# An encoder block on one core: the projection's first block in another order, outer products stored by SP, the first head's K and Q loaded at other places

## What is computed

```python
proj = rmsnorm(h, norm1_g) @ w_in                # 1024 -> 2048: q, k, v, u, 512 columns each
lam = exp(sum(lam_q1 * lam_k1)) - exp(sum(lam_q2 * lam_k2)) + 0.2
p = softmax(q_i . k_i * 64**-0.5 - slope_h * |i - j|)            # i = 0, 1: two maps per head
att = rmsnorm((p[0] - lam * p[1]) @ v, subln_g) * 0.8
ssm = bi_s5_glu(u, ...)              # two scans, 32 groups of 64 complex states, then GELU and a gate
h = h + concat(att, ssm) @ w_out
h = h + square(relu(rmsnorm(h, norm2_g) @ w_mlp1)) @ w_mlp2
return rmsnorm(h, final_g)
```

## Time and profile before

| | |
|---|---|
| median of 3 runs | 2672.96 us (2672.41 to 2673.84) |
| the profiled execution | 2665.66 us, its span 2663.5 us |
| PE busy | 2548.7 us, 96% of the span |
| DVE, ACT, POOL busy | 2077.4, 1416.7, 389.5 us |
| DMA | 397.18 MB, mean 149 GB/s |

### The profile page before, as it was taken

How to read it: one execution, slowest core, us unless ns; L and a number is a source line. 1 busy time by engine, 2 the same in 40 slices (tenths; PEclk the granted TensorE clock), 3 DMA queues, 4 the chain that set the end, 5 groups by cost and what they waited for, 6 DMA issues and landing times.

```text
span 2663.5 us, 32920 instructions
## 1 busy us (share of the span) xinstructions
PE 2548.7 (96%) x12804; PEld 2079.2 (78%) x12804; DVE 2077.4 (78%) x2074; ACT 1416.7 (53%) x1753; POOL 389.5 (15%) x333
## 2 busy tenths in 40 slices
PE   7998999999999988988989999999999999999997
PEld 6886777877787877766777888888887888888886
DVE  5866657999999968766998876777889877678885
ACT  5276626777787762224434666533345565643334
POOL 3410021212121113310434000000014000000003
PEclk9999999999999999998999999999999999999999
DMA  5356542020213119966665554452234664452211
GB/s 187 119 188 221 216 136 72 25 64 26 56 39 89 49 41 255 256 220 245 221 236 202 212 206 186 174 205 106 104 109 159 233 221 174 181 198 95 97 78 63
DMA packets 162714, 397.18 MB, mean 149 GB/s; under 512 B 29568, under 2 KB 87168, under 8 KB 134784
## 3 DMA queue, kind: packets, MB, share of 16 engines
q1 hardware_dynamic: 145856, 319.07, 36.1%
q10 hardware_dynamic: 16704, 76.03, 7.2%
HBM read 270.79 MB, written 122.16 MB: 148 GB/s over the span
## 4 chain that ended last, share of the span: by engine, by line
PE 45%; DVE 3%; POOL 1%; issue 1%; DMA 0%; ACT 0%; SPq 0%; DVEq 0%; ACTq 0%; POOLq 0%
PE ml_bank L2590 15%; PE ml_bank L2592 15%; PE ml_bank L2591 15%; POOL kp_tabs L2199 1%; DVE ml_res L2470 1%; DMA kp_low<-hn_s 0%; DVE ml_hb L2504 0%; DVE ml_b_split L2401 0%; DVE ml_w_split L2412 0%; DVE ml_res L2490 0%; DVE ml_rinv L2496 0%; PE ml_bank L2598 0%; DVE kp_low L2425 0%; DVE kp_tabs L2446 0%; DVE ml_t_first L2419 0%
## 5 line engine op out<-in xcount | busy, mean ns | idle before, releaser
L2590 PE MATMUL ml_bank<-ml_b_split,ml_w_split 128*128 128x512 f32 x2016 | 788.8, 391 | 9.7 <-issue 9.4
L2591 PE MATMUL ml_bank<-ml_b_split,ml_w_split 128*128 128x512 f32 x2016 | 786.1, 390 | 0.0
L2592 PE MATMUL ml_bank<-ml_b_split,ml_w_split 128*128 128x512 f32 x2016 | 785.9, 390 | 0.0
L2590 PEld LDWEIGHTS ml_bank<-ml_b_split,ml_w_split 128*128 128x128 f32 x2016 | 379.5, 188 | 93.2 <-issue 14.1
L2591 PEld LDWEIGHTS ml_bank<-ml_b_split,ml_w_split 128*128 128x128 f32 x2016 | 379.6, 188 | 79.9 <-issue 1.2
L2592 PEld LDWEIGHTS ml_bank<-ml_b_split,ml_w_split 128*128 128x128 f32 x2016 | 379.6, 188 | 79.1
L1065 ACT ACTIVATE at_e<-at_e,at_neg_top 128x2048 f32<-128x2048 f32 x128 | 256.5, 2004 | 143.2 <-DVE at_neg_top L1119 143.2
L2199 POOL TENSOR_TENSOR kp_tabs<-kp_tabs,ml_square 128x512 f32<-128x512 f32 x55 | 144.2, 2622 | 1265.8 <-ACT ml_square L2303 1259.3
L2470 DVE TENSOR_TENSOR ml_res<-ml_bank,ml_res 128x2048 f32<-128x2048 f32 x75 | 171.5, 2287 | 118.7 <-PE ml_bank L2592 118.7
L2237 ACT ACTIVATE ml_b_split<-kp_u_t 128x2048 fp32r<-128x2048 f32 x54 | 103.5, 1917 | 300.5 <-PE ml_bank L2592 300.5
L1221 PEld LDWEIGHTS pj_banks<-at_v,at_a_t 128*128 128x128 f32 x2048 | 238.6, 192 | 22.8 <-issue 22.6
(11 more groups left out here) (227 smaller groups left out, 4057.3 us busy)
## 6 DMA issues: line engine op xcount, KB each, us to landing
act_s<-ml_res ACTq DMA_DIRECT2D x32, 1024.0 KB, 4.2
kp_wide<-in_w_stream SPq DMA_DIRECT2D x18, 1024.0 KB, 5.1
kp_bp<-in_w_stream SPq DMA_DIRECT2D x18, 1024.0 KB, 5.8
kp_tabs<-in_w_stream SPq DMA_DIRECT2D x18, 1024.0 KB, 6.7
ml_r<-in_w_stream SPq DMA_DIRECT2D x18, 1024.0 KB, 6.8
tab_s<-kp_tabs ACTq DMA_DIRECT2D x32, 512.0 KB, 3.0
kp_low<-hn_s SPq DMA_DIRECT2D x16, 1024.0 KB, 5.6
kp_u_t<-hn_s SPq DMA_DIRECT2D x16, 1024.0 KB, 4.8
```

What stands on the lines that cost most here:

```text
L2590: pe.matmul(out, w_hi[:, w], b_hi[:, b], start=fresh and kt == 0, stop=False, skip_group_check=True)
L2591: pe.matmul(out, w_hi[:, w], b_lo[:, b], start=False, stop=False, skip_group_check=True)
L2592: last = pe.matmul(out, w_lo[:, w], b_hi[:, b], start=False, stop=kt == 3, skip_group_check=True)
```

## The change

It has five parts.

1. **Opening.** ACT runs a small activation before it waits for data. The first slice of x is a DMA of its own ahead of the first weight piece, and is split first. PE runs eight matmuls of 128 by 128 on the constant `ones`.
2. **Block 0.** Strip 1 of x is loaded behind weight piece 6 instead of ahead of it. ACT takes the inverse norm's root (`stats(0)`) after piece 6, and splits piece 7 in the middle of block 1's squares; DVE splits piece 7 after the evacuation of group 1. `rates` and `chunk_turns` move from groups 2 and 3 to ahead of `invert(0)`, `magnitudes` to behind the split of x for block 1.
3. **Outer products** are stored by SP, right behind the store of their own group.
4. **First K.** It is loaded behind group 53's store into the first half of `e`, and ACT splits it in one run with Q 0 and 1 before it evacuates group 56; DVE's `first_k_low`, the biases and the lambda exponents move two or one groups ahead.
5. **Q 2 and 3** are issued behind group 62's store; the wait for all stores of u moves into attention, ahead of the first load of u.

```diff
     def store_outer(self, sp, i):
-        act.wait_ge(self.outer_ready, i + 1)
+        sp.wait_ge(self.outer_ready, i + 1)
 ...
+        sp.dma_start(x_raw[:, 0], x_tiles[:, 0, 0:TB]).then_inc(x_first_loaded, 16)
         load_w(0)
-        load_half_x(0, 0)
+        sp.dma_start(x_raw[:, 1:KD // 2], x_tiles[:, 1:KD // 2, 0:TB]).then_inc(x_loaded[0], 16)
 ...
-            if i == HALF_W - 2:
+            if i == HALF_W - 1:
                 load_x(1)
 ...
             store(n)
-            if n == NG - 8:
+            if n in PREP_OUTERS:
+                prep.store_outer(sp, PREP_OUTERS.index(n))
+            if n == NG - 11:
 ...
+            if n == NG - 2:
+                for tile in range(2, 4):
+                    attention.load_q(sp, tile)
 ...
-        for i in range(2):
-            sp.wait_ge(qku_stored[i], 16 * (SECOND + NV * NTB) // 2)
 ... (ACT)
+        act.activation(rms_t[:, 0:1], eps_c[:], ACT.Copy)
+        split_x(0, range(1))
         split_w(0)
-        split_x(0)
+        split_x(0, range(1, KD))
 ...
+        prep.time_steps(act)
+        split_w(6)
         stats(0)
-        prep.time_steps(act)
-        squares(1, range(KD))
-        prep.magnitudes(act)
+        squares(1, range(KD // 2))
+        split_w(7)
+        squares(1, range(KD // 2, KD))
 ...
+            if n == NGROUP - 1:
+                prep.magnitudes(act)
 ...
-            if n == NG - 7:
+            if n == NG - 9:
                 prep.all_used(act)
-                attention.k_high(act, 0, range(4))
+                attention.q_high(act, 0)
+                attention.k_high(act, 0, range(8))
+                attention.q_high(act, 1)
 ...
-            if n - 2 in PREP_OUTERS:
-                prep.store_outer(act, PREP_OUTERS.index(n - 2))
 ... (DVE)
-        for i in range(1, HALF_W):
+        for i in range(1, HALF_W - 1):
             split_w(i)
+        prep.rates(dve)
+        prep.chunk_turns(dve)
         invert(0)
 ...
+            if n == 1:
+                split_w(HALF_W - 1)
 ... (PE)
+        for i in range(8):
+            pe.matmul(stat_b[:, 0:P], ones[:], ones[:], start=True, stop=True)
 ... (attention)
+        self.k_raw = [self.e[:, 0]] + [later_k] * (H - 1)
```

More of the change, by code:

```diff
@@ L639, in split_w, with split_x @@
             act.activation(w_hi[:, :, w_slot(i)], w_raw[:, i % 2], ACT.Copy).then_inc(w_hi_ready, 1)
-        def split_x(b):
+        def split_x(b, ks=range(KD)):
             x = BLOCK_X[b]
-            for k in range(KD):
-                if k % (KD // 2) == 0:
+            for k in ks:
+                if x == 0 and k == 0:
+                    act.wait_ge(x_first_loaded, 16)
+                elif x == 0 and k == 1 or k % (KD // 2) == 0:
                     act.wait_ge(x_loaded[k // (KD // 2)], 16 * (x + 1))
@@ L685, in _ @@
         squares(0, range(3, 5))
-        for i in range(3, HALF_W):
+        for i in range(3, 6):
             split_w(i)
-            if i < 6:
-                squares(0, range(i + 2, i + 3))
+            squares(0, range(i + 2, i + 3))
+        prep.time_steps(act)
+        split_w(6)
         stats(0)
-        prep.time_steps(act)
-        squares(1, range(KD))
-        prep.magnitudes(act)
+        squares(1, range(KD // 2))
+        split_w(7)
+        squares(1, range(KD // 2, KD))
         act.wait_ge(rinv_ready, 1)
@@ L755, in prepare @@
         def prepare(n):
-            if n == 2:
-                prep.rates(dve)
-            elif n == 3:
-                prep.chunk_turns(dve)
-            elif n == 8:
+            if n == 8:
                 prep.first_power(dve)
@@ L869, in _, with u_written @@
             evacuated(pe, last)
-    return block, attention
+    def u_written(eng):
+        for i in range(2):
+            eng.wait_ge(qku_stored[i], 16 * (SECOND + NV * NTB) // 2)
+    return block, attention, u_written
 class Attention:
@@ L1224, in values, with phase_attention @@
             last.then_inc(self.pv_done, 1)
-def phase_attention(block, a, head):
+def phase_attention(block, a, u_written, head):
     NQ, NS, QB = a.NQ, a.NS, a.QB
@@ L2712, in encoder_block @@
             with ExitStack() as early:
-                block, attention = phase_project(
+                block, attention, u_written = phase_project(
                     nc, early, shared, x_t, norm1_g, w_in, qk_s, v_s, u_s, (s_par, s_bc, mag, tab_s, bp_s, cp_s),
                     (lam_in, att_s, att_square, att_floor))
-                phase_attention(block, attention, head)
+                phase_attention(block, attention, u_written, head)
             phase_ssm(nc, head, following, mag, s_d, w_glu, b_glu, z_s, ssm_s, att_s, att_square, att_floor, gains, att_t)
```

35 lines of the change are left out of this document (17 added, 18 removed).

## The result

The changed kernel takes 2637.22 us (median of 4 runs, 2634.68 to 2639.76), the kernel before 2672.68 us (4 runs, 2667.49 to 2673.84). The ratio is 0.9871, 95% interval [0.9854, 0.9888]: 1.3% faster, 35.5 us by the medians. Measured again later, it gave 2636.66 us (2634.82 to 2639.88), ratio 0.9876 [0.9859, 0.9892]. The profiled execution took 2638.42 us, 27.2 us less than that of before. The forecast was 2641.0 (2630 to 2658). In us the interval of the first ratio is a gain of 29.9 to 39.0; the forecast gain was 32.2.

The account below looks back on a forecast made before the run. PE, busy 96% of the span, was taken to bound the kernel, so only its waits up to 420 us counted. Six terms summed to 32.2 us off the 2672.96 us median, giving 2640.8, say 2641 us, range 2630 to 2658.

Parts of the forecast that it names:

- opening: Start of the kernel: first matmul sooner, but group 1 still waits for its low weight; 1.2 us, bounds 0 and 2.8.
- block 0's end: Before block 1: earlier weight piece 6, root and rates remove PE's waits of 1.6 and 4.5 us; 7.7 us, bounds 3 and 7.7.
- block 4 to 5: Outer products: SP's earlier store shrinks block 5's stall from 10.5 to about 6 us; 4.5 us, bounds -3 and 12.1.
- block 5 to 6: Outer products again: earlier store removes the 2.5 us stall and 1.6 us of slow clock; 4.1 us, bounds 0 and 4.1.
- K: First scores: earlier load removes PE's 6.1 us wait for K's low part and 1.6 us slow clock; 7.7 us.
- Q 2: Tile 2's scores: earlier load starts them 4.5 us sooner, with 2.5 us of slow clock gone; 7.0 us.
- rival A: SP's queue takes back the outer products' gain through late weight piece 14; gain 23.6 us, 2649.4 us; chance 0.14.
- B: The first phase absorbs its own gain, PE waiting 8.9 us longer at block 5; gain 23.3 us; chance 0.09.
- C: Slower: SP as one queue is late with everything, losing 40 us on PE; 2689 us; chance 0.04.
- D: The seam does not gain: K's transfer or POOL ends as late as before; gain 24.5 us; chance 0.07.
- E: Outer products: only ACT's issue slots count, the two stalls shrink 0.9 us each; gain 25.4 us; chance 0.05.
- three signs of being wrong: Block 5 stall over 10 us; PE waiting for low weights in groups 36 to 39; attention and S5 growing by projection's gain.

Follow-up runs that it names:

- e6: The changed kernel without its whole opening (no matmuls on ones, no early activation, first x slice not ahead of the first weight): 2639.01 us, ratio 0.9892.
- e2: The kernel before with only the opening and block 0's end changed; outer products, K and Q as before: 2662.74 us, ratio 0.9969 to before.
- e1: The kernel before with only the outer products' stores moved to SP, behind the group's own store: 2662.35 us, ratio 0.9965 to before.
- e3: The changed kernel with the first K and all Q loads put back where they were before: 2653.85 us, ratio 0.9938 to before.
- e7: The changed kernel with only Q 2 and 3 loaded where they were before, first K still early: 2642.73 us, ratio 0.9899 to before.
- e4: The changed kernel with outer product 1 stored by SP one group later, behind the load of weight piece 14: 2632.25 us, ratio 0.9861 to before.

## Why the prediction held, and where a term was off

The forecast missed the median by 3.8 us, on the side of too little gain; the path says the opposite, 29.5 us where 32.2 were forecast. By its own steps, each term is set against the difference of consecutive milestones (the second groups of blocks 1, 5 and 6; K: to the scores of tile 1, which carry no slow clock; Q 2: to the row of 421.11 in the earlier trace rows, at 391.66 now):

| term | forecast | measured |
|---|---|---|
| opening | 1.2 | 0.7 (group 1 at 16.48, 17.21 before); nothing that lasts (e6) |
| block 0's end | 7.7 | 8.1; without SP's stores 5.3 at the state step, opening included (e2) |
| block 4 to 5 | 4.5 | 2.4 (1.9 to 3.0 in the other executions); alone 3.2, or 3.9 from block 1 on (e1) |
| block 5 to 6 | 4.1 | 3.5, 0.6 us of stall is left; 3.8 alone (e1) |
| K | 7.7 | 7.8; 8.2 by e3 and e7 |
| Q 2 | 7.0 | 7.0; 7.2 by e7 |
| sum | 32.2 | 29.5 |

**Right in mechanism and size:** block 0's end, K and Q. Weight piece 6 is split at 30.17 us (near 30 forecast), the split of piece 7 waits 0.57 us, and `x_hi` of block 1 waits for PE. Tile 2's scores are released by DVE's bias steps, as said, with 1.2 us of wait. The head start passes through attention: 28.2 us at tile 2's scores, 30.7 at the state step.

**Right in mechanism, wrong in size: the outer products.** Apart from PE's head start, outer product 2 was to start some 1 us sooner, outer product 3 some 3.6 and `x_hi` 4.5. Less the 8.9 us of head start at block 1, they came 0.4 us sooner (211.74 against 220.98), 2.1 (225.81 against 236.79) and 2.6 (242.35 against 253.81). The term was mis-sized at 4.5, with 2.4 measured. Most is lost between the two outer products. The 4.1 us ahead of the issue went as forecast: SP issues the store at 218.58, when DVE is done, and it lands 3.9 us later. But outer product 3 does not start then. DVE first idles 3.86 us for the angles of ACT's table and makes a table step, so from the start of outer product 2 to that of 3 it takes 14.07 us where it took 15.81: 1.7 us less, and not 2.6. The restart was mis-sized too. The prediction took eight slow matmuls, 1.6 us; behind block 5's stall the four executions of this code have 9 to 14 of them and lose 2.0 to 3.0 us, before 1.8. The prediction had named what eats it, piece 14 behind SP's wait for outer product 1, and priced it too low: ACT idled 9.44 us for it, and e4 got 5.4 us back (second group of block 5 at 246.11; 5.8 counted from block 1) by moving one store. With it, the term is 2.4 + 5.4 = 7.8, within the bound of 12.1. I had listed rival A as all or nothing at 0.14; it held in part, and its condition, that outer product 2 hangs on piece 15's split, was the true one: it starts 1.0 us behind that split's low part in the changed kernel, in e1 and in e4. Before, it was the store that it waited for, and the prediction did not ask why that store took 11.8 us to land: it said that the transfer is not faster from SP, and it landed in 6.0, ahead of the x strip.

**The opening** rested on group 1 waiting for its low weight, which is right, and on that weight being no later than before, which is not: it is ready at 16.43 us instead of 15.89, since x slice 0 ahead of it splits DVE's work and makes it wait.

**The rivals.** A in part, see above. B in part: alone, block 0's gain loses 2.2 us at block 5. C, D and E fell: the wait of SP that matters cost 5.4 us, not 40; K gained 8.2 by e3 and e7; e1 gained 6.5 at the state step where E gives 1.8. None of the three signs of being wrong is there: the stall at block 5 is 7.9 us, PE waits for no weight's low part in groups 36 to 39, and attention and S5 do not grow by what the projection gains.

**The whole.** At the state step the changed kernel is 30.7 us ahead (30.1 in its second execution); the profiled executions end 27.2 apart, the medians 35.5, and 32.2 in the second comparison. That the forecast lies near the medians is luck in part: on the path the gain is 1.5 to 2.7 us less than forecast, and the first pair of medians gives 3.3 us more. Behind the state step, the time varies by more than these differ, as the spans of 230.7 to 239.7 us show. PE's waits for DMA in the whole execution show one part of it, for before, the changed kernel and e1:

```profile
PE sm_y_ps L1815 <- DMA sm_toeplitz<-sm_strip: 4.1, 3, 2.9
PE sm_lag_ps L1791 <- DMA kp_low<-cp_s: 2.3, 1, 2.3
PE sm_turn_ps L1778 <- DMA kp_bp<-bp_s: 1.4, 1, 1.4
```

```profile
PE sm_y_ps L1834 <- DMA sm_toeplitz<-sm_strip: 4.4, 3, 1.8
PE sm_turn_ps L1797 <- DMA kp_bp<-bp_s: 4.1, 1, 4.1
PE sm_lag_ps L1810 <- DMA sm_cp<-cp_s: 0.4, 1, 0.4
```

```profile
PE ml_bank L2622 <- DMA ml_gain<-in_gains: 7.5, 1, 7.5
PE sm_turn_ps L1778 <- DMA kp_bp<-bp_s: 3.1, 1, 3.1
```

Whether some of the 35.5 us is a gain behind the state step can't be told from these runs; I leave it open.

## What to carry to other kernels

Moving a DMA to an engine that has nothing else to do removes the wait for its place in a program, but the wait for its data then stands ahead of everything else in the new queue: look at what is loaded right behind it, and put that load first (5.4 us here for one moved line). Where a stall is short, the engine's restart at the lower clock can cost nearly as much as the stall: removing the last 2.3 us brought 3.9. Judge parts of a long kernel by milestones that repeat, and the whole by medians: here a phase that nobody touched differed by 6.5 us between two executions of one kernel, and by 9 us over all.

## What I had not expected of the hardware

How long the slow pace lasts behind a stall isn't settled by the stall's length. Up to block 5 the changed kernel, its repetition, e3 and e7 are the same code, and their stalls there are alike (7.87, 7.38, 7.12, 7.44 us). Yet the group behind takes 7.5, 8.1, 7.6 and 8.4 us, where one at full clock takes 5.4. Behind the short stalls at block 6 the slow matmuls begin at another place: behind 2.50 us in before the first three microseconds were granted 0.51, behind 2.49 us in e2 0.63. The price is the same, as the two groups take 7.1 and 7.2 us.

```profile
303.40:306.40 3.00, 2.98 (x7) 0.51 0.77 316
```

```profile
297.60:300.60 3.00, 2.98 (x9) 0.63 0.76 316
```

POOL's low parts of K take 10.35 us for four, where four took 5.44 in the earlier trace rows. In that time DVE makes the first biases, from the same buffer `e` as far as the rows tell. In before, POOL's low parts of Q took 5.02 us for two beside the same step of DVE, and 0.98 for two without it. PE doesn't wait for POOL here (POOL, then DVE), and what slows it wasn't tried.

```profile
346.84 10.35 POOL L1066 TENSOR_TENSOR at_k_lo<-at_e,at_k_hi 64x512 fp32r<-64x512 f32 x4 [1.19 <-ACT at_k_hi L1058]
...
347.32 4.35 DVE L1172 SCALAR_TENSOR_TENSOR at_bias<-at_e 128x2048 f16<-128x2048 int32 x2
```
